# A weight ring of eight buffers for the first block, with its chunks in order of use

## The reference, cut to what matters

```python
mod = silu(c) @ w_ada + b_ada            # 6144 columns; the same for c_ctx
h  = modulate(rmsnorm(x),   shift, scale)       # needs mod columns 0..2047
hc = modulate(rmsnorm(ctx), shift_c, scale_c)
# context: k, v, a of hc -> final states s_f, s_b of both directions
# tokens: q, k, v, g, a, p = split(h @ w_in)
la = log_sigmoid(a @ w_dec + b_dec) / 16        # decays, then chunked linear attention
o  = rmsnorm(scores @ v + q @ state) * silu(g)  # 4 heads, two directions
x  = x + gate * (concat([o, pooled(p) @ w_pool]) @ w_out)
h2 = modulate(rmsnorm(x), shift_m, scale_m)     # then router and 32 experts, top 2
```

## Time and profile before

| what | value |
|---|---|
| median of three runs | 1272.95 us |
| profiled execution, its own time | 1272.7 us |
| its span, first to last instruction | 1270.9 us |
| TensorE busy | 1161.5 us, 91% of the span |
| VectorE busy / ScalarE busy | 670.6 us, 53% / 498.7 us, 39% |
| chain that ended last: TensorE's share | 73% |
| mean granted TensorE clock | 0.949 of full |
| HBM read | 256.05 MB, 202 GB/s over the span |

### The profile page before, as it was taken

How to read it: one execution, slowest core, us unless ns; L and a number is a source line. 1 busy time by engine, 2 the same in 40 slices (tenths; PEclk the granted TensorE clock), 3 DMA queues, 4 the chain that set the end, 5 groups by cost and what they waited for, 6 DMA issues and landing times.

```text
span 1270.9 us, 19640 instructions
## 1 busy us (share of the span) xinstructions
PE 1161.5 (91%) x8302; PEld 978.4 (77%) x8302; DVE 670.6 (53%) x1045; ACT 498.7 (39%) x759; POOL 0.2 (0%) x4
## 2 busy tenths in 40 slices
PE   4698696989999999689999999799999999999986
PEld 2487584864555555479999987699889999999985
DVE  1546234442333333555755586857755677555666
ACT  2572113231111111354444363234883455434452
POOL 0000000000000000000000000000000000000000
PEclk9798877989999999899999998899999999999988
DMA  8521254789999997336444523233234655455320
GB/s 349 231 100 67 98 201 166 277 349 421 421 420 421 421 388 279 120 118 243 178 165 188 184 100 133 91 107 127 89 123 165 222 175 187 179 199 194 122 82 34
DMA packets 38156, 258.42 MB, mean 203 GB/s; under 512 B 4368, under 2 KB 5136, under 8 KB 7856
## 3 DMA queue, kind: packets, MB, share of 16 engines
q1 hardware_dynamic: 36720, 252.90, 51.7%
q10 hardware_dynamic: 1344, 4.21, 0.9%
HBM read 256.05 MB, written 1.05 MB: 202 GB/s over the span
## 4 chain that ended last, share of the span: by engine, by line
PE 73%; DVE 6%; ACT 2%; issue 2%; DVEq 0%; ACTq 0%
PE bank L516 72%; DVE wl L1690 1%; ACT wh L1181 1%; DVE acc L1736 1%; DVE xt L1727 0%; PE bank L876 0%; DVE rstd L1714 0%; DVE hl L1741 0%; DVE arena L2231 0%; ACT L1191 0%; DVE small L2230 0%; PE bank L834 0%; PE bank L779 0%; DVE arena L1883 0%; DVE xt L2416 0%
## 5 line engine op out<-in xcount | busy, mean ns | idle before, releaser
L516 PE MATMUL bank<-hh,wh 128*128 128x256 f32 (+1 forms) x1256 | 368.2, 293 | 9.2 <-DVE hl L1741 6.2
L516 PE MATMUL bank<-hl,wh 128*128 128x256 f32 (+1 forms) x1256 | 362.3, 288 | 0.0
L516 PE MATMUL bank<-hh,wl 128*128 128x256 f32 (+1 forms) x1256 | 361.9, 288 | 0.0
L1690 DVE TENSOR_TENSOR wl<-raw,wh 128x1024 fp32r<-128x1024 f32 (+4 forms) x246 | 277.9, 1168 | 138.1 <-ACT wh L1181 136.8
L1181 ACT ACTIVATE wh<-raw 128x1024 fp32r<-128x1024 f32 (+4 forms) x246 | 236.2, 1006 | 104.6 <-PE bank L516 77.9
L516 PEld LDWEIGHTS bank<-hh,wh 128*128 128x128 f32 x1256 | 245.2, 195 | 16.2 <-issue 13.2
L516 PEld LDWEIGHTS bank<-hl,wh 128*128 128x128 f32 x1256 | 245.3, 195 | 2.2 <-issue 0.8
L516 PEld LDWEIGHTS bank<-hh,wl 128*128 128x128 f32 x1256 | 244.8, 195 | 1.2
L516 PE MATMUL bank<-yh,wh 128*128 128x256 f32 x512 | 147.3, 288 | 5.4 <-DVE yl L1710 3.7
L516 PE MATMUL bank<-yl,wh 128*128 128x256 f32 x512 | 146.7, 287 | 0.0
L516 PE MATMUL bank<-yh,wl 128*128 128x256 f32 x512 | 146.5, 286 | 0.0
(11 more groups left out here) (233 smaller groups left out, 1363.8 us busy)
## 6 DMA issues: line engine op xcount, KB each, us to landing
raw<-in_gu SPq DMA_DIRECT2D x40, 1024.0 KB, 15.3
raw<-in_w_ada SPq DMA_DIRECT2D x24, 1024.0 KB, 6.9
arena<-in_gu SPq DMA_DIRECT2D x24, 1024.0 KB, 14.6
raw<-in_gd SPq DMA_DIRECT2D x22, 1024.0 KB, 13.4
raw<-in_f1g SPq DMA_DIRECT2D x11, 1024.0 KB, 5.2
raw<-in_f2g SPq DMA_DIRECT2D x11, 1024.0 KB, 4.8
raw<-in_f2u SPq DMA_DIRECT2D x11, 1024.0 KB, 4.8
raw<-in_f2d SPq DMA_DIRECT2D x11, 1024.0 KB, 4.9
```

Source lines behind the costliest of these rows:

```text
L516: return pe.matmul(o, l, m, start=start, stop=stop, skip_group_check=True)
L1690: v.tensor_tensor(WL[slot_of[U]][:, 0:n], src, WH[slot_of[U]][:, 0:n].bitcast(f32), ALU.subtract).then_inc(S("wl"), 1)
```

## The change

The output activations YH and YL (3072 columns each) are now laid next to each other, and three raw buffers of 2048 columns, `early0` to `early2`, lie over the same memory. With `raw4`, whose own use starts later, and `raw0` to `raw3` that makes a ring of eight for the first eight chunks, which wait for nothing. From the ninth chunk on the ring has five (`raw0` to `raw3` and `early1`, called BETWEEN), six once `raw4` has joined at `w1g 1`; BETWEEN leaves before the experts. The first writers of the lent memory (ScalarE for YH, VectorE for YL, ScalarE for PTM) get a wait for the borrowed chunks. YH and YL are split into a part of 8 and a part of 4 tiles (YHA, YLA) so that the lent parts are whole; the later users get new offsets.

The chunk list is put in the order in which TensorE eats it: ada 2 before `w1ak 0`, ada 3 before `w1ak 1`, ada 4 before `w1v 1`. TensorE takes ada 4 before v 1, ada 5 and turn 4 before turn_keys, g 0 before states 2, g 1 before states 1, ada 7 and ada 8 earlier by one place, and head_norm 1 only after w_op 0. PSUM banks are dealt anew for that. ScalarE's five loads of constants stand behind the second root instead of before `ada_row(1)`; `w1ak 1` is split in the middle of the modulation loop instead of ahead of the second root; the splits of g, w_op and w_og stand elsewhere between the copies.

```diff
@@ -80,7 +80,8 @@
         NR, NU, AHEAD = 5, 6, 4
-        raw_in = [cx.enter_context(nc.semaphore(f"raw_in{i}")) for i in range(NR + 11)]
+        raw_in = [cx.enter_context(nc.semaphore(f"raw_in{i}")) for i in range(NR + 12)]
+        raw_in = raw_in + [raw_in[NR], raw_in[NR + 1]]
         bank_out = {p: [cx.enter_context(nc.semaphore(f"{p}bank_out{i}")) for i in range(8)] for p in ("", "x_")}
...
@@ -106,15 +107,17 @@
         XT = XTt[:, :].rearrange("p (k t) -> p k t", k=8)
-        YHt, YLt = sb("yh", [128, 3072], f32r), sb("yl", [128, 3072], f32r)
+        with ExitStack() as outer:
+            YHt, YLt = (outer.enter_context(nc.sbuf_tensor(n, [128, 3072], f32r)) for n in ("yh", "yl"))
+        EARLY = [sb(f"early{i}", [128, 2048]) for i in range(3)]
         wide = lambda T: T[:, :].rearrange("p (k t) -> p k t", k=8)
...
         H0, L0, H1, L1 = half(HHt, 0), half(HLt, 0), half(HHt, 1), half(HLt, 1)
-        YH = YHt[:, :].rearrange("p (k t) -> p k t", k=12)
-        YL = YLt[:, :].rearrange("p (k t) -> p k t", k=12)
+        YH, YHA = YHt[:, 0:2048].rearrange("p (k t) -> p k t", k=8), YHt[:, 2048:3072].rearrange("p (k t) -> p k t", k=4)
+        YL, YLA = YLt[:, 1024:3072].rearrange("p (k t) -> p k t", k=8), YLt[:, 0:1024].rearrange("p (k t) -> p k t", k=4)
         CS = sb("csts", [128, co["scanm"][0]])
...
@@ -199,13 +202,13 @@
         RSXa = ar(2666, 256)
-        RAW += [ar(3072 + 2048 * i, 2048) for i in range(5)]
+        RAW += [ar(3072 + 2048 * i, 2048) for i in range(5)] + [EARLY[1], EARLY[0], EARLY[2]]
         CAP = 64
...
         PG = [YHt[:, 2048 + 512 * i:2560 + 512 * i].rearrange("p (a s) -> p a s", a=2) for i in range(2)]
-        PT = [YLt[:, 2048 + 512 * i:2560 + 512 * i].rearrange("p (j t) -> p j t", j=2) for i in range(2)]
-        YGH, YGL = (T[:, 0:2048].rearrange("p (j f) -> p j f", j=2) for T in (YHt, YLt))
+        PT = [YLt[:, 512 * i:512 * i + 512].rearrange("p (j t) -> p j t", j=2) for i in range(2)]
+        YGH, YGL = (T.rearrange("p (j f) -> p j f", j=2) for T in (YHt[:, 0:2048], YLt[:, 1024:3072]))
         IDR = PG[1][:, 0, 0:128]
...
@@ -248,13 +251,14 @@
 
-        add_ada(0, 1)
+        add_ada(0, 1, 2)
         add("w1ak", 0)
-        add("w1ak", 1)
-        add_ada(2, 3)
-        for n, i in [("p", 0), ("p", 1), ("q", 0), ("v", 0), ("v", 1)]:
+        add_ada(3)
+        for n, i in [("ak", 1), ("p", 0), ("p", 1), ("q", 0), ("v", 0)]:
             add("w1" + n, i)
-        add_ada(4, 5)
+        add_ada(4)
+        add("w1v", 1)
+        add_ada(5)
         add("w1g", 0)
...
@@ -298,19 +302,25 @@
         late = where["w1ak", 0]
-        eaten[late:late + 6] = [late + 4, late + 5, late, late + 1, late + 2, late + 3]
+        eaten[late:late + 3] = [late + 2, late, late + 1]
 
...
         first_e, last_e = where["gu", 0], where["gd", 31]
-        EXTRA_W, EXTRA_A = range(NR, NR + 6), range(NR + 6, NR + 11)
-        raw_of, raw_no, raw_last, follows = [], [], [-1] * len(RAW), []
-        ring = collections.deque(range(NR - 1))
+        EXTRA_W, EXTRA_A, BETWEEN, EARLY_H, EARLY_L, POOLS = range(NR, NR + 6), range(NR + 6, NR + 11), NR + 11, NR + 12, NR + 13, NR - 1
+        raw_of, raw_no, raw_last, follows, loads = [], [], [-1] * len(RAW), [], {}
+        ring = collections.deque([POOLS, EARLY_H, EARLY_L, 0, 1, 2, 3, BETWEEN])
         for c in range(len(chunks)):
+            if c == 8:
+                first_in = {r: raw_last[r] for r in (POOLS, EARLY_H, EARLY_L)}
+                for r in first_in:
+                    ring.remove(r)
             if c == where["w1g", 1]:
-                ring.appendleft(NR - 1)
+                ring.appendleft(POOLS)
             if c == first_e:
+                last_between = raw_last[BETWEEN]
+                ring.remove(BETWEEN)
                 ring.extendleft(reversed(EXTRA_A[:4]))
...
             follows.append(raw_last[r])
-            raw_no.append(1 + raw_no[raw_last[r]] if raw_last[r] >= 0 else 1)
+            shared = {EARLY_H: NR, EARLY_L: NR + 1}.get(r, r)
+            loads[shared] = loads.get(shared, 0) + 1
+            raw_no.append(loads[shared])
             raw_last[r] = c
...
@@ -382,21 +394,20 @@
         fixed((("p", 0), 6), (("p", 1), 7), (("pool", 0), 1), (("pool", 1), 6), ("q", 7), (("v", 0, 0), 1), (("v", 0, 1), 6))
-        fixed((("poolw", 0), 7), (("poolw", 1), 1), (("v", 1, 0), 6), (("v", 1, 1), 7))
+        fixed((("poolw", 0), 7), (("poolw", 1), 1), (("ada", 4), 7), (("mod", 1), 3), (("v", 1, 0), 6), (("v", 1, 1), 1), (("ada", 5), 7))
         fixed((("kt", 0), 2), (("kt", 1), 4), (("kt", 2), 5), (("kt", 3), 0))
-        put = over([1, 6, 7, 2, 4, 5, 0])
+        put = over([7, 6, 1, 2, 4, 5, 0])
         st_jobs = lambda j: put(*[("st", j, x) for x in range(4)])
-        put(("ada", 4))
-        job(("mod", 1), 3)
         st_jobs(0)
-        put(("scr", 0), ("ada", 5))
+        put(("scr", 0), ("g", 0))
         st_jobs(2)
-        put(("scr", 1), ("g", 0), ("o", 0))
+        put(("scr", 1), ("ada", 6), ("o", 0), ("g", 1))
         st_jobs(1)
-        put(("scr", 2), ("ada", 6), ("o", 1))
+        put(("scr", 2), ("o", 1), ("ada", 7))
         st_jobs(3)
-        put(("scr", 3), ("g", 1), ("o", 2), ("gn", 0), ("ada", 7), ("o", 3), ("ada", 8), ("gn", 1))
-        put(("wo", 0), ("wo", 1), ("ada", 9), ("wo", 2), ("wo", 3), ("wo", 4), ("wo", 5))
+        put(("scr", 3), ("o", 2), ("gn", 0), ("ada", 8), ("o", 3))
+        put(("wo", 0), ("wo", 1), ("gn", 1), ("ada", 9), ("wo", 2), ("wo", 3), ("wo", 4))
+        job(("wo", 5), jobs["gn", 1][1])
         job("w_stat", 3)
...
@@ -646,6 +657,7 @@
                 t.then_inc(S("poolw"), 1)
+            ada_rows(4)
             lin_tm(("w1v", 1), [take(pe, ("v", 1, 0)), take(pe, ("v", 1, 1))], 4, HW, LW)
...
@@ -722,36 +734,35 @@
 
+            ada_rows(5)
+            turn(4)
             for j in range(4):
                 turn_keys(j)
-            ada_rows(4)
             states(0)
             scores(0)
-            turn(4)
-            ada_rows(5)
+            turn(5)
+            lin_fm(("w1g", 0), [take(pe, ("g", 0))], HX, LX)
             states(2)
             scores(1)
-            turn(5)
-            lin_fm(("w1g", 0), [take(pe, ("g", 0))], HX, LX)
+            ada_rows(6)
             outs(0)
+            lin_fm(("w1g", 1), [take(pe, ("g", 1))], HX, LX)
+            turn(6)
             states(1)
             scores(2)
-            ada_rows(6)
             outs(1)
-            turn(6)
+            ada_rows(7)
             states(3)
             scores(3)
-            lin_fm(("w1g", 1), [take(pe, ("g", 1))], HX, LX)
+            turn(7)
             outs(2)
             head_norm(0)
-            ada_rows(7)
+            ada_rows(8)
             outs(3)
-            turn(7)
-            ada_rows(8)
-            head_norm(1)
             turn(8)
...
             mix_out("w_op", 0, wo0, range(4), False)
+            head_norm(1)
             ada_rows(9)
...
@@ -1227,11 +1238,6 @@
                     ada_row(0)
-            a.dma_start(POOLM.rearrange("p a g t -> p (a g t)"), D["cst"][:, co["pool"][0]:co["pool"][1]]).then_inc(S("d_a0"), 16)
-            a.dma_start(WPOOL.rearrange("p g d -> p (g d)"), D["w_pool"]).then_inc(S("d_a0"), 16)
-            a.dma_start(SCM, D["cst"][:, co["scanm"][0]:co["scanm"][1]]).then_inc(S("d_g"), 16)
-            a.dma_start(GLM.rearrange("p a t -> p (a t)"), D["cst"][:, co["glam"][0]:co["glam"][1]]).then_inc(S("d_g"), 16)
-            a.dma_start(WDEC[0:32, :], D["w_dec"]).then_inc(S("d_g"), 16)
             ada_row(1)
...
             through("w1ak", 0)
-            through("w1ak", 1)
             a.wait_ge(*nth("xn", 4))
             root("statc", "sqc_used", 8)
+            a.dma_start(POOLM.rearrange("p a g t -> p (a g t)"), D["cst"][:, co["pool"][0]:co["pool"][1]]).then_inc(S("d_a0"), 16)
+            a.dma_start(WPOOL.rearrange("p g d -> p (g d)"), D["w_pool"]).then_inc(S("d_a0"), 16)
+            a.dma_start(SCM, D["cst"][:, co["scanm"][0]:co["scanm"][1]]).then_inc(S("d_g"), 16)
+            a.dma_start(GLM.rearrange("p a t -> p (a t)"), D["cst"][:, co["glam"][0]:co["glam"][1]]).then_inc(S("d_g"), 16)
+            a.dma_start(WDEC[0:32, :], D["w_dec"]).then_inc(S("d_g"), 16)
             ada_row(2)
...
@@ -1255,6 +1265,8 @@
                 a.activation(HC[:, k, :], CT[:, k, :], ACT.Identity, scale=A1[:, 1, k:k + 1], bias=B1[:, 1, k:k + 1]).then_inc(S("hc_h"), 1)
+                if k == 3:
+                    through("w1ak", 1)
             through("w1p", 0)
...
@@ -1307,11 +1321,14 @@
             decay_exps(3)
+            given_back(a, first_in[EARLY_H])
             for gq in range(2):
...
                 a.activation(YH[:, 2 * gq:2 * gq + 2, :], PY[:, 2 * gq:2 * gq + 2, :], ACT.Copy).then_inc(S("yp_h"), 1)
+            ada_row(4)
             through("w1g", 0)
             values_in(1)
+            ada_row(5)
             for j in range(4):
...
             through("w1g", 0)
             values_in(1)
```

(29 more changed lines are left out.)

17 lines of the change are left out of this document (10 added, 7 removed).

## The result

The changed kernel takes 1240.8 us (median of 4 runs, 1239.11 to 1242.8) where the kernel before takes 1271.61 (median of 4) beside it: a ratio of 0.975, with a 95% interval of 0.9715 to 0.9785. The profiled execution took 1242.8 us, with a span of 1241.0 against 1270.9. Repeated twice on other occasions, the change gave medians of 1242.98 and 1243.62.

The account below looks back on a forecast made before the run. It took TensorE's waits for late loads (buffers, not bandwidth) and row copies, before about 250 us, as the bound. Terms 8.9 + 10.0 + 11.8 - 0.7 = 30.0 off 1272.7 gave 1242.7 us, range 1234 to 1256.

Parts of the forecast that it names:

- Term 1: The start, up to mod being read: ada 2 and ada 3 no longer wait for loads, 8.9 us gained.
- rival B: Start: SP's backlog of loads holds x back to about 24 us instead of 17.4; 1249 us, chance 0.07.
- From ak to the pool weights ... only shifts: Stretch from ak to the pool weights: nothing moved but ada 4, so it only starts earlier, with no gain of its own.
- Term 2: Middle, v 1 to g 0: `w1g 0` loads earlier, so states 0 starts sooner; 10.0 us, between 9.2 and 10.8.
- Term 3: Outs 0 to turn 8: 44.4 us against 56.2, the waits of turns 7 and 8 gone; 11.8 us gained.
- Term 4: Output product, w_op 0 to w_og 1, with head_norm 1 behind w_op 0: 29.0 us instead of 28.3, so -0.7.
- D: The clock gains: start and outs (terms 1 and 3) at their upper ends; 1236 us, chance 0.06.
- C: The slow clock spreads over the light work from turn 6 to turn 8: 1257 us, half of it 1250; chance 0.13.
- E: No difference: the stream of gu and gd, not TensorE, sets the experts' end; time stays 1272 us, chance 0.04.
- F: Slower: TensorE at half clock from v 1 to w_og; 1288 us with 45 us more at half, chance 0.03.

Follow-up runs that it names:

- e1_five: The change with a ring of five buffers from the start instead of eight, all else as in the change: 1240.14 us, ratio 0.9747.
- e9_four_start: The change with only four buffers for the first eight chunks, the fifth from the ninth chunk on: 1242.14 us, ratio 0.9762.
- e3_old_order: The change's buffers and start, but from the pool weights on the kernel before's order of work, chunks and banks: 1247.7 us, ratio 0.9801.

## Why the prediction was right, and where its reasons were not

The sum was 30.0 us and 29.98 were measured at w_stat, with nothing behind it changed. By its own steps:

- **Term 1**, forecast 8.9, measured 9.79 at ak and 9.60 at ada 4. Ada 2 and ada 3 without waits, VectorE's chain as the next in line, mod read at 40.22 against 40.7: right. x did not land 0.4 later but 0.3 earlier (17.15), as the whole start of this profile lay 0.3 earlier, and between 16.78 and 17.57 in all kernels with the new list; rival B is out. Where its reasons fail is its first sentence: it puts the gain down to eight free loads. Five give it too (`e1_five`), and so do four with the fifth buffer for the last half of ada 3 (`e9_four_start`), because ada 0 hands its two back at 12 to 13 us. What is needed is the new order and a fifth buffer; 2.1 of the 9.8 go with the moved split of `w1ak 1`, for which 1.6 were counted.
- **"From ak to the pool weights ... only shifts"** held in the sum alone: +1.46 in ak and +1.50 behind it from the clock, -1.50 for a longer wait and -1.69 in the pool products, in this profile.
- **Term 2**, forecast 10.0, measured 10.57, near the upper of its two values (10.8), since states 0 ran at the full clock. The mechanism as put, that `w1g 0` comes early because ada 4 moves ahead of v 1, is what the trace of the change shows (ada 4 ends at 114.65, the load goes out at 114.72), but it is not needed: with ada 4 at its old place the load went out at 108.00 and the wait was gone (e3_old_order). The fifth buffer is enough.
- **The rule in term 2.** The row shows states 0 at full speed, 3.05 us in a window at 1.00, behind 1.95 us of transposes and a wait of 1.21. The Trainium skill, "TensorE: Matmul & The Clock Gate", Part 4, says that transpose mode does not count as PE-busy in the same way. From that a low clock at states 0, and a term of 9.2, was worked out, and the trace does not bear it out here: the transposes and states 0 both ran at 1.00. How the chip counts them is not shown.
- **Term 3**, forecast 11.8, measured 11.35, in part by luck, as two errors cancel. Of the three waits named (1.4 before head_norm 0, 0.5 before outs 2, 1.1 before turn 8) the first did not come: ScalarE did stand 6.94 us for `w_op 1`, but outs 2 took 7.1 us at the lower clock and covered it. The others were 0.72 and 0.42. That made 0.9 us less idle than the 2 counted. The slow clock cost more than the 5.5 kept: of 44.97 us from ada 6 to turn 8, 36.9 are work at full rate and 1.15 idle, which leaves 6.9.
- **Term 4**, forecast -0.7, measured -1.54: w_op 0 was given the full clock (5.8 us) and took 7.5, four of them in a window at 0.57; the waits (0.76 and 0.62, together 1.4) were a little shorter than the 1.8 counted.
- **Rivals.** D and C are both a little true: the clock gained in ak and lost in the pool products, the outs and w_op 0. The four terms are off by +0.7, +0.6, -0.4 and -0.8, so that the sum is closer than its parts were known. E and F are out: the stream of gu began at 207.34 instead of 237.32, and the experts' stage took its 227 us (226.18 busy, 0.96 DMA share).

So the number was right, and two of the causes behind it were not those that were named. Of the 30 us, by w_stat: 22.4 are kept in the kernel with the old order of work (249.76 less 227.35). Of these 9.4 are there at ak, from the new order of the chunks with the fifth buffer and the moved split, and 13.0 come behind, where the fifth buffer is enough. The new order of work adds 5.0 to 7.6 on top; alone it may be worth more, as it too would free `w1g 0`. The three further buffers lent at the start are nothing.
